# Expert weights slot by slot instead of in groups of four slots, in a Mamba-2, GLA and PEER trunk layer on one Trainium2 core

## The chip, the cores and the metric

The kernel runs on one core of a Trainium2 chip. The metric is the device time of one execution in microseconds; less is better. The names of the engines in the rows: PE is TensorE's matmuls (PEld its weight loads), DVE is VectorE, ACT is ScalarE, POOL is GpSimd, SP is SyncE, which issues transfers only. A q behind a name is the engine's instruction queue.

## The reference

One layer is applied to 1024 new tokens (the prompt) and to 8 single tokens (the samples): a modulated RMSNorm, a mixer (16 Mamba-2 heads beside 4 gated linear attention heads), a residual, a second modulated RMSNorm, and an expert layer (PEER) with its residual and a last RMSNorm. All of it is in 32-bit floats. The change touches the expert layer alone:

```python
def block_fn(xb):                                   # 128 tokens
    qd = (xb @ w_query).reshape(-1, PEER_HEADS, 2, PEER_DQ // 2)
    s1 = jnp.einsum('thd,hkd->thk', qd[:, :, 0], sub_keys1)
    s2 = jnp.einsum('thd,hkd->thk', qd[:, :, 1], sub_keys2)
    v1, i1 = lax.top_k(s1, 16); v2, i2 = lax.top_k(s2, 16)
...                                                 # the best 16 of the 256 sums, for each of 8 heads
    g = jax.nn.softmax(top_s, axis=-1)
    u = expert_down[idx]
    act = jax.nn.gelu(jnp.einsum('thkd,td->thk', u, xb), approximate=False)
    return jnp.einsum('thk,thkd->td', g * act, expert_up[idx])
```

So each token picks 8 x 16 = 128 experts out of 16384. An expert is one row of `expert_down` and one of `expert_up`, 1024 numbers each.

## The kernel before

Five phases follow one another, with a barrier between them: modulation and first norm, the input projections, the mixer for the samples, the mixer for the prompt, and the experts. Each phase has one program per engine, and semaphores tie the programs together; each engine works through its own program in order.

The expert phase (`experts`) goes over the prompt in 8 tiles of 128 tokens, one token per partition, tile 0 written out and tiles 1 to 7 in a hardware loop on each engine, and then over the 8 samples. A tile has 128 **slots**: slot k is the k-th chosen expert of each of the 128 tokens. For each slot

- GpSimd gathers 128 rows, one per token, of 2048 numbers (down row and up row side by side, 8 KB) into one of 8 buffers (`buf`, a ring of `RING = 8`) with one indirect DMA (L1764). It waits for `summed`, which says that the slot eight places earlier has been used up (L1769).
- VectorE multiplies the down halves with the tokens and sums them, one dot per token (`dot`, L1866), as soon as the gather has landed. It increments `dotted`.
- ScalarE turns the dots into weights. `GROUP = 4` slots go together: it waits for the fourth dot of the group (L1835), computes the gelu of all four columns in one instruction (L1836), multiplies each column by its gate (L1838, four instructions), and writes for each slot a diagonal matrix with the 128 weights (L1842, a copy of the identity scaled per partition) into a ring of 8. Each diagonal increments `weighed`. Where ScalarE reads what it has just written, `Chain.step` makes it wait for its own write.
- TensorE waits for `weighed` of the slot and adds diagonal x up halves to two PSUM banks (L1797, two matmuls of 512 columns, which appear as four records). Its last matmul increments `summed`.

Between groups, the same engines do the routing of the next tile in pieces, so many after each group as hand-written tables say (`PE_PIECES`, `ACT_PIECES`, `DVE_PIECES`): TensorE the query products (L1528), the token transposes (L1509) and scores (L1520) after groups 1 to 13; ScalarE the copies out of PSUM (L1544, L1554, L1549) and two exponentials (L1564); VectorE the searches for the best 16 after groups 8 to 27. At the start of a tile, VectorE reads the previous tile's sum out of PSUM after its fourth dot (`fin.add`, f_y, L1662); TensorE's first slot waits for it. ScalarE computes the last norm of the previous tile after group 0 (`fin.scalar`). SyncE loads the tokens (h2) and the residual (x1) of a tile and stores its output (y).

The samples use the same buffers: sample b is one slot of 128 rows, and its dot, gelu (L1857), weights and matmuls (L1815) go slot by slot already.

Of the kernel before, what the change touches and what calls it, by code (L numbers as in the profile page):

```python
# [21 lines left out]
ACT = mybir.ActivationFunctionType  # L22
# [22 lines left out]
SLOTS = PH * TOPK  # L45
RING = 8
GROUP = 4
# [57 lines left out]
class Prog:  # L105
# [31 lines left out]
    def sem(self, name):  # L137
        handle = self.nc.alloc_semaphore(name=name)
        self.sems.append(handle)
        return handle  # L140
# [1551 lines left out]
def drive(pieces, count):  # L1692

    for _ in range(count):
        next(pieces, None)


def experts(g):
# [4 lines left out]
    NG = SLOTS // GROUP  # L1703
    with ExitStack() as st:
# [4 lines left out]
        idx, gate, h2 = sb("idx", [P, SLOTS], U32), sb("gate", [P, SLOTS]), sb("h2", [P, D])  # L1709
        dots, acts, wts = sb("dots", [P, SLOTS]), sb("acts", [P, SLOTS]), sb("wts", [P, SLOTS])  # L1710
# [3 lines left out]
        dotted, wch, weighed, summed = sem("dotted"), sem("wch"), sem("weighed"), sem("summed")  # L1714
# [13 lines left out]
        @block.sync  # L1728
        def _(sp):
            sp.sem_inc(fin.stored, 16)  # L1730
            sp.dma_start(rt.h2[:], g.h2_d[0:P, :]).then_inc(rt.h2_in, 16)
            rt.load_constants(sp)
            sp.dma_start(fin.gate2[:], g.mod_d[NS, 5 * D:6 * D].partition_broadcast(P)).then_inc(fin.consts_in, 16)
            sp.dma_start(fin.final[:], io["norm_final"].partition_broadcast(P)).then_inc(fin.consts_in, 16)

            def store_y(n):
                sp.wait_ge(fin.y_ready, n + 1)
                sp.dma_start(io["y_p"][bass.ds(n * P, P), :], fin.y[:]).then_inc(fin.stored, 16)

            def tile(n, first):  # L1740
                sp.wait_ge(h2_kept, n + 1)
                sp.dma_start(rt.h2[:], g.h2_d[bass.ds(n * P + P, P), :]).then_inc(rt.h2_in, 16)
                if not first:
                    store_y(n - 1)
                sp.dma_start(fin.x1[:], g.x1_d[bass.ds(n * P, P), :]).then_inc(fin.x1_in, 16)

            tile(0, True)
            with sp.Fori(1, NT) as n:
                tile(n, False)
            sp.wait_ge(rt.q_ps, 4 * (NT + 1))  # L1750
            for b in range(NS):
                sp.dma_start(spread(b), g.h2_d[SEQ + b, :].partition_broadcast(P)).then_inc(spread_in, 16)
            sp.wait_ge(fin.sum_read, NT)
            sp.dma_start(fin.gate2[0:NS, :], g.mod_d[0:NS, 5 * D:6 * D]).then_inc(gates_in, 16)
            store_y(NT - 1)
            sp.dma_start(fin.x1[0:NS, :], g.x1_d[SEQ:ROWS, :]).then_inc(fin.x1_in, 16)
            sp.wait_ge(fin.y_ready, NT + 1)
            sp.dma_start(io["y_s"], fin.y[0:NS, :]).then_inc(fin.stored, 16)
            sp.wait_ge(fin.stored, 16 * (NT + 2))
# [60 lines left out]
        @block.scalar  # L1820
        def _(act):
            A = nc.scalar.activation
            own = rt.scalar(act, 0)
            drive(own, 10)
            def tile(n, first):
                ch = Chain(act, wch, n * (2 + 2 * NG))
                route = rt.scalar(act, n + 1)
                for q in range(NG):
                    if q in (0, NG // 2):
                        half = 0 if q == 0 else 1  # L1830
                        gs = slice(half * HALF_SLOTS, (half + 1) * HALF_SLOTS)
                        act.wait_ge(rt.gated, n * 2 + half + 1)
                        ch.step(A(gate[:, gs], rt.gate[:, gs], ACT.Copy))
                    ks = slice(q * GROUP, (q + 1) * GROUP)
                    act.wait_ge(dotted, n * SLOTS + (q + 1) * GROUP)  # L1835
                    ch.step(A(acts[:, ks], dots[:, ks], ACT.Gelu))  # L1836
                    for k in range(q * GROUP, (q + 1) * GROUP):
                        last = A(wts[:, k:k + 1], acts[:, k:k + 1], ACT.Copy, scale=gate[:, k:k + 1])  # L1838
                    ch.step(last)
                    for k in range(q * GROUP, (q + 1) * GROUP):  # L1840
                        act.wait_ge(summed, n * SLOTS + k + 1)
                        A(diag[:, k % RING, :], g.ident[:], ACT.Copy, scale=wts[:, k:k + 1]).then_inc(weighed, 1)  # L1842
                    if first:
                        drive(own, FIRST_ACT_PIECES.get(q, 0))
                    drive(route, ACT_PIECES.get(q, 0))
                    if q == 0 and not first:
                        fin.scalar(act, n - 1, P)

            tile(0, True)
            with act.Fori(1, NT) as n:  # L1850
                tile(n, False)
            act.wait_ge(turn_ps, 1)
            A(turned[:].rearrange("p a b -> p (a b)"), g.bank(2, cols=2 * NS), ACT.Copy).then_inc(turn_kept, 1)
            fin.scalar(act, NT - 1, P)
            for b in range(NS):
                act.wait_ge(s_dotted, b + 1)
                A(wts[:, b:b + 1], dots[:, b:b + 1], ACT.Gelu).then_inc(s_acted, 1)  # L1857
            fin.scalar(act, NT, NS)
# [135 lines left out]
```

## Time and profile before

| | |
|---|---|
| time, median of 3 runs | 4351.11 us (4350.53 to 4353.85) |
| profiled execution, its own time | 4346.83 us |
| its span in the trace | 4345.3 us |
| mean granted TensorE clock | 0.894 of full speed |
| expert slots of the prompt, first to last | about 1398 to 4310 us of the span |
| data moved | 1268.44 MB, of it 1114.83 MB by GpSimd's queue |

An engine's busy time is the time in which its instructions ran. In a row of instructions the tile names stand as out<-in with x and a count, then busy time and mean duration, then the idle time of the engine before these instructions and what ended it. The granted clock is a share of TensorE's full 2.4 GHz; its lower level is 1.2 GHz, 0.50.

### The profile page before, as it was taken

To read this page: it belongs to the slowest core of one execution; us is meant where nothing else is said; L and a number is where in the kernel's file an instruction comes from. 1 tells how busy PE (TensorE), PEld (TensorE's weight loads), DVE (VectorE), ACT (ScalarE), POOL (GpSimd) and SP (SyncE) were. 2 spreads that over 40 slices of the span, in tenths; PEclk is the share of its full clock that TensorE was granted. 3 is DMA by queue.
4 is the path that set the end of the run, shared out by engine and by line. 5 is a ranking of instruction groups with operands and counts; after the bars stand their busy time and mean duration, and the time that the engine had idled before them with its cause. 6 is when DMAs were issued, how large, how long until landed. Compare 5 with 4: busy or idle time off the path is not lost.

```text
span 4345.3 us, 39670 instructions
## 1 busy us (share of the span) xinstructions
PE 3465.6 (80%) x11665; PEld 1919.4 (44%) x11665; DVE 2356.5 (54%) x4736; ACT 1058.9 (24%) x3031; POOL 1357.3 (31%) x1251
## 2 busy tenths in 40 slices
PE   5998994679994987787797787788779778877876
PEld 1997772255553533442353253244335325334432
DVE  4531104556654766467457546646745754664674
ACT  2110112134431222222222222222222222222222
POOL 1110111200000444444344343444434434444342
PEclk8999995789997998898898898889889889989988
DMA  7332212453224999999999999999999999999996
GB/s 289 95 110 102 82 43 93 170 187 105 87 72 192 368 375 364 379 383 373 368 386 375 381 373 371 376 373 379 374 364 393 377 377 380 378 370 378 395 375 265
DMA packets 210786, 1268.44 MB, mean 292 GB/s; under 512 B 26081, under 2 KB 51305, under 8 KB 74138
## 3 DMA queue, kind: packets, MB, share of 16 engines
q0 software_dynamic: 159760, 1114.83, 65.1%
q1 hardware_dynamic: 50834, 151.67, 9.8%
q14 instruction: 147, 1.20, 0.1%
q8 instruction: 45, 0.74, 0.1%
HBM read 1218.12 MB, written 48.29 MB: 291 GB/s over the span
## 4 chain that ended last, share of the span: by engine, by line
PE 27%; DMA 25%; issue 8%; ACT 3%; POOL 3%; DVE 3%; POOLq 0%; ACTq 0%; DVEq 0%; SPq 0%
DMA e_buf<-in_experts,e_idx 25%; PE ps L1797 23%; PE ps L1528 4%; POOL e_buf L1764 3%; ACT e_wts L1838 2%; DVE e_buf L1866 2%; ACT e_diag L1842 1%; ACT e_acts L1836 1%; DMA e_buf<-in_experts,e_idxT 0%; DVE r_row L1617 0%; DVE r_work L1616 0%; DMA r_wq<-in_w_query 0%; POOLq L58 0%; DVE r_work L1613 0%; PE ps L1815 0%
## 5 line engine op out<-in xcount | busy, mean ns | idle before, releaser
L1797 PE MATMUL ps<-e_buf,e_diag 128*128 128x512 f32 x4096 | 2045.7, 658 | 628.3 <-ACT e_diag L1842 627.7
L1866 DVE SCALAR_TENSOR_TENSOR e_buf<-e_buf,e_h 128x1024 f32<-128x1024 f32 x1024 | 1247.7, 1226 | 1098.7 <-DMA e_buf<-in_experts,e_idx 1084.2
L1764 POOL DMA_INDIRECT e_buf<-in_experts,e_idx x1024 | 1200.1, 1172 | 1612.2 <-PE ps L1797 1411.0
L1797 PEld LDWEIGHTS ps<-e_buf,e_diag 128*128 128x128 f32 x4096 | 843.1, 211 | 1759.6 <-issue 999.9
L1836 ACT ACTIVATE e_acts<-e_dots 128x4 f32<-128x4 f32 x256 | 52.6, 205 | 2087.6 <-DVE e_buf L1866 2087.5
L1842 ACT ACTIVATE e_diag<-ident,e_wts 128x128 f32<-128x128 f32 x1024 | 327.2, 390 | 25.8
L1528 PEld LDWEIGHTS ps<-r_h2T,r_wq 128*128 128x128 f32 x2304 | 269.3, 193 | 34.0 <-issue 34.0
L1528 PE MATMUL ps<-r_h2T,r_wq 128*128 128x128 f32 x2304 | 269.9, 276 | 3.0 <-DMA r_wq<-in_w_query 3.0
L856 PE MATMUL ps<-xo_w_out,xo_catT 128*128 128x512 f32 x512 | 224.5, 592 | 1.7 <-DVE xo_x L889 1.7
L1838 ACT ACTIVATE e_wts<-e_acts,e_gate 128x1 f32<-128x1 f32 x1024 | 218.6, 284 | 10.1 <-ACT e_acts L1836 2.2
L74 PE MATMUL ps<-p_wth,hT_high 128*128 128x512 f32 (+1 forms) x432 | 170.6, 395 | 10.9 <-PEq L439 10.9
L76 PE MATMUL ps<-p_wth,hT_low 128*128 128x512 f32 (+1 forms) x432 | 171.0, 396 | 0.0
L75 PE MATMUL ps<-p_wtl,hT_high 128*128 128x512 f32 (+1 forms) x432 | 170.4, 395 | 0.0
L74 PE MATMUL ps<-hT_high,p_wh 128*128 128x344 f32 x480 | 154.7, 322 | 11.4 <-DVE p_wl L69 11.4
L76 PE MATMUL ps<-hT_high,p_wl 128*128 128x344 f32 x480 | 154.2, 321 | 0.0
L75 PE MATMUL ps<-hT_low,p_wh 128*128 128x344 f32 x480 | 154.0, 321 | 0.0
L856 PEld LDWEIGHTS ps<-xo_w_out,xo_catT 128*128 128x128 f32 x512 | 96.7, 190 | 117.6 <-issue 117.2
L907 POOL DMA_DIRECT2D x_d<-xo_x x8 | 4.3, 541 | 411.4 <-DVE xo_x L889 411.4
L64 DVE CAST p_wth<-p_wt 128x4096 fp32r<-128x4096 f32 x6 | 13.8, 2292 | 199.1 <-PE ps L76 190.7
L610 POOL DMA_DIRECT2D proj_d<-p_ev x54 | 31.6, 585 | 280.8 <-ACT p_ev L645 280.8
L645 ACT ACTIVATE p_ev<-ps 128x512 f32<-128x512 f32 (+1 forms) x54 | 32.3, 598 | 280.2 <-PE ps L76 280.2
L74 PEld LDWEIGHTS ps<-hT_high,p_wh 128*128 128x128 f32 x480 | 91.0, 190 | 12.3 <-DVE p_wl L69 12.3
(353 smaller groups left out, 2971.1 us busy)
## 6 DMA issues: line engine op xcount, KB each, us to landing
m_w<-in_w_mod SPq DMA_DIRECT2D x12, 2048.0 KB, 9.0
e_buf<-in_experts,e_idx POOLq DMA_INDIRECT x1024, 9.2
p_wt<-in_w_rows SPq DMA_DIRECT2D x6, 2048.0 KB, 8.3
proj_d<-p_ev POOLq DMA_DIRECT2D x48, 256.0 KB, 2.3
x_zgv<-proj_d SPq DMA_DIRECT2D x8, 1536.0 KB
p_w<-in_w_chan SPq DMA_DIRECT2D x20, 512.0 KB, 4.1
r_wq<-in_w_query SPq DMA_DIRECT2D x4, 2048.0 KB, 14.1
xbc_d<-p_res POOLq DMA_DIRECT2D x12, 516.0 KB, 3.0
```

Source lines behind the costliest of these rows:

```text
L74: nc.tensor.matmul(out, lhsT[0], rhs[0], start=start, stop=False)
L75: nc.tensor.matmul(out, lhsT[0], rhs[1], start=False, stop=False)
L76: return nc.tensor.matmul(out, lhsT[1], rhs[0], start=False, stop=stop)
L645: nc.scalar.activation(evs[n % 6][0:rs, :], g.bank(n % 6, rows=rs), func).then_inc(tevac, 1)
L856: last = g.nc.tensor.matmul(g.bank(cols, rows=rs), self.catT[:, k, 0:rs], self.w[:, k, cols * 512:(cols + 1) * 512], start=(k == 0), stop= ...
L1528: last = nc.tensor.matmul(g.bank(4 + b, cols=P, at=m * P), self.wq[:, b, k, m * P:(m + 1) * P], self.h2T[:, k, :], start=(k == 0), stop=(k ...
L1764: return pool.indirect_dma_start(out=buf[s][:], out_offset=None, in_=io["experts"], in_offset=bass.IndirectOffsetOnAxis(ap=numbers, axis=0 ...
L1797: last = nc.tensor.matmul(g.bank(cols), diag[:, k % RING, :], buf[k % RING][:, D + cols * 512:D + (cols + 1) * 512], start=(k == 0), stop= ...
L1836: ch.step(A(acts[:, ks], dots[:, ks], ACT.Gelu))
L1838: last = A(wts[:, k:k + 1], acts[:, k:k + 1], ACT.Copy, scale=gate[:, k:k + 1])
L1842: A(diag[:, k % RING, :], g.ident[:], ACT.Copy, scale=wts[:, k:k + 1]).then_inc(weighed, 1)
L1866: V.scalar_tensor_tensor(out=down, in0=down, scalar=1.0, in1=row, op0=ALU.mult, op1=ALU.mult, accum_out=out).then_inc(sem, 1)
```

## The change

ScalarE no longer handles four slots at a time. For each slot it waits for that slot's dot, computes the gelu of the one column, multiplies it by the gate, and writes the diagonal; each of the first two is followed by a wait for its own write. The count of such waits per tile rises from 2 + 2 x 32 to 2 + 2 x 128. The routing pieces stay where they were, after every fourth slot, and the other engines' programs are as before.

```diff
             def tile(n, first):
-                ch = Chain(act, wch, n * (2 + 2 * NG))
+                ch = Chain(act, wch, n * (2 + 2 * SLOTS))
...
-                    ks = slice(q * GROUP, (q + 1) * GROUP)
-                    act.wait_ge(dotted, n * SLOTS + (q + 1) * GROUP)
-                    ch.step(A(acts[:, ks], dots[:, ks], ACT.Gelu))
                     for k in range(q * GROUP, (q + 1) * GROUP):
-                        last = A(wts[:, k:k + 1], acts[:, k:k + 1], ACT.Copy, scale=gate[:, k:k + 1])
-                    ch.step(last)
-                    for k in range(q * GROUP, (q + 1) * GROUP):
+                        act.wait_ge(dotted, n * SLOTS + k + 1)
+                        ch.step(A(acts[:, k:k + 1], dots[:, k:k + 1], ACT.Gelu))
+                        ch.step(A(wts[:, k:k + 1], acts[:, k:k + 1], ACT.Copy, scale=gate[:, k:k + 1]))
                         act.wait_ge(summed, n * SLOTS + k + 1)
                         A(diag[:, k % RING, :], g.ident[:], ACT.Copy, scale=wts[:, k:k + 1]).then_inc(weighed, 1)
```

## Rows read from the trace of the kernel before

**Rows 1.** The page: busy time of each engine, share of the span.
```profile
PE 3465.6 (80%) x11665; PEld 1919.4 (44%) x11665; DVE 2356.5 (54%) x4736; ACT 1058.9 (24%) x3031; POOL 1357.3 (31%) x1251
```
**Rows 2.** The page: the chain that ended last, shares by line.
```profile
DMA e_buf<-in_experts,e_idx 25%; PE ps L1797 23%; PE ps L1528 4%; POOL e_buf L1764 3%; ACT e_wts L1838 2%; DVE e_buf L1866 2%; ACT e_diag L1842 1%; ACT e_acts L1836 1%; DMA e_buf<-in_experts,e_idxT 0%; DVE r_row L1617 0%; DVE r_work L1616 0%; DMA r_wq<-in_w_query 0%; POOLq L58 0%; DVE r_work L1613 0%; PE ps L1815 0%
```
**Rows 3.** Busy time by stretch: length, engines, granted clock, DMA share, GB/s.
```profile
1397.93:3928.82 2530.89, 2007.58 (x5648) 976.95 (x5649) 1536.60 (x3497) 637.11 (x2180) 1053.36 (x909) 0.89 0.95 376
2121.85:2280.95 159.10, 135.37 (x508) 76.75 (x507) 85.33 (x185) 42.80 (x142) 65.46 (x57) 0.93 0.96 380
2280.95:2481.99 201.04, 148.38 (x301) 61.53 (x300) 130.72 (x300) 48.54 (x171) 81.54 (x73) 0.89 0.95 376
3273.00:3297.00 24.00, 23.59 (x103) 14.40 (x102) 11.92 (x21) 5.28 (x19) 10.29 (x10) 1.00 1.00 417
2148.00:2164.00 16.00, 9.26 (x23) 4.36 (x22) 6.63 (x11) 3.25 (x10) 4.28 (x5) 0.80 1.02 429
2136.00:2144.00 8.00, 8.00 (x14) 3.21 (x13) 5.21 (x9) 6.01 (x13) 3.50 (x3) 0.71 0.59 218
2176.00:2184.00 8.00, 8.00 (x43) 5.47 (x42) 3.52 (x6) 2.94 (x10) 3.07 (x3) 1.00 0.98 367
4320.00:4328.00 8.00, 5.65 (x12) 0.83 (x12) 4.78 (x12) 0.61 (x3) 0.00 (x0) 1.00 1.01 426
```
**Rows 4.** The chain in order of time: start us, us, what.
```profile
2211.74 10.82 DMA e_buf<-in_experts,e_idx
...
2223.86 0.21 ACT e_acts L1836
...
2224.14 0.15 issue
2224.29 0.66 ACT e_wts L1838 x3
...
2225.51 7.15 PE ps L1797 x16
...
2233.42 10.40 DMA e_buf<-in_experts,e_idx
```
**Rows 5.** Timeline of TensorE in the sample part: start us, us, instruction, idle before.
```profile
4325.85 1.88 PE L1815 MATMUL ps<-e_buf,e_wpad 128*8 128x512 f32 x4 [0.55 <-DVE e_wpad L1906]
4328.28 1.88 PE L1815 MATMUL ps<-e_buf,e_wpad 128*8 128x512 f32 x4 [0.55 <-DVE e_wpad L1906]
```
**Rows 6.** The page: groups of ScalarE, busy and mean ns, then idle before.
```profile
L1836 ACT ACTIVATE e_acts<-e_dots 128x4 f32<-128x4 f32 x256 | 52.6, 205 | 2087.6 <-DVE e_buf L1866 2087.5
L1842 ACT ACTIVATE e_diag<-ident,e_wts 128x128 f32<-128x128 f32 x1024 | 327.2, 390 | 25.8
...
L1838 ACT ACTIVATE e_wts<-e_acts,e_gate 128x1 f32<-128x1 f32 x1024 | 218.6, 284 | 10.1 <-ACT e_acts L1836 2.2
```
**Rows 7.** Timeline at the start of tile 2.
```profile
2121.03 0.70 DVE L1876 COPY e_h<-r_h 128x1024 f32<-128x1024 f32 x1 [3.90 <-issue]
...
2132.69 1.22 DVE L1662 TENSOR_TENSOR f_y<-ps,f_gate 128x1024 f32<-128x1024 f32 x1
...
2134.46 17.03 PE L1797 MATMUL ps<-e_buf,e_diag 128*128 128x512 f32 x32 [8.51 <-ACT e_diag L1842]
...
2145.41 0.95 POOL L1764 DMA_INDIRECT e_buf<-in_experts,e_idx  x1 [0.77 <-PE ps L1797]
```
**Rows 8.** Timeline of TensorE amid the router's pieces, tile 2.
```profile
2179.18 3.73 PE L1528 MATMUL ps<-r_h2T,r_wq 128*128 128x128 f32 x32
2182.75 7.03 PE L1797 MATMUL ps<-e_buf,e_diag 128*128 128x512 f32 x16
2189.62 3.73 PE L1528 MATMUL ps<-r_h2T,r_wq 128*128 128x128 f32 x32
...
2210.80 1.05 PE L1520 MATMUL ps<-r_keys,r_qT 128*128 128x128 f32 x8
```
**Rows 9.** The page: DMA issues of the gathers, median us to landing.
```profile
e_buf<-in_experts,e_idx POOLq DMA_INDIRECT x1024, 9.2
```

## Prediction

> **What bounds the kernel now.** The page's engine line first [rows 1]: no engine is full over the span (PE 80%, with matmuls of which part ran at half clock; VectorE 54%, ScalarE 24%). The chain that ended last [rows 2] is mostly two things in turn, transfers of gathered experts (25%) and the L1797 matmuls (23%), with ScalarE and GpSimd pieces between. A chain that alternates like this is a loop through several engines, so I read the time of one turn.
>
> The stretches [rows 3] give the size: seven tiles take 2530.89 us, 361.6 us a tile, 2.82 us a slot, at 376 GB/s. A slot gathers 128 rows of 8 KB, 1.049 MB. DMA share is 0.95 there, which looks full, but the share does not measure what is left: at shares of 1.00 to 1.02 the same engines moved 417, 429 and 426 GB/s, and at 0.98 only 367. Where a tile starts and little is left to fetch, 8 us fall to 218.
>
> The chain in order of time [rows 4] shows the turn. The gather issued at 2211.74 lands after 10.82 us; then its dot, one gelu, three further gate products, the first diagonal, and 16 matmuls (the four slots of the group), 7.15 us, until GpSimd issues the gather that reuses this buffer, at 2233.42. That is 21.68 us for a ring of eight slots: 2.71 us a slot. Eight transfers back to back, spaced as in the sample part, where nothing holds the gathers up (2.43 us from one slot's matmuls to the next) [rows 5], need only 19.4 us. So the ring is the limit, not the transfer: a group keeps four buffers of eight until its fourth dot is there.
>
> **The change, part by part.** *Removed:* the wait of slots 0 to 2 of a group for slot 3, and batching. On the turn in [rows 4] three gate products (0.66 us) leave the path before the first diagonal, and of the 16 matmuls 12 (three quarters of 7.15, 5.36 us) have been done while the later transfers landed. The turn falls from 21.68 to about 15.7 us, under the 19.4 us that eight transfers need. The transfers themselves become the limit; the spare 3.7 us becomes queueing, so issue-to-landing, now a median of 9.2 us [rows 9], should rise to about 13 us.
>
> *Added on ScalarE:* gelu of one column instead of four. A 4-column one takes 205 ns [rows 6]; 96 more a tile, 768 in all, are 157 us of busy time, and each gate product now waits for its own gelu (0.15 us of "issue" in [rows 4], some 0.1 ms in all if every one counted). Cover: ScalarE sat idle 2087.5 us for dots [rows 6]. A slot will cost it 0.2 + 0.28 + 0.39 plus about 0.3 of waits, 1.2 us of the 2.5 available. Were the cover gone, the price would be those 157 us and the waits. Queued behind the new wait for each dot are the later diagonals, the router's copies and exponentials and the finishing norm; all of these already stood behind the group's last dot, so none gets later, nor do PE and VectorE, which wait for them. The added waits for the chain semaphore are on ScalarE's own results only.
>
> *Moved:* the gathers, which GpSimd issues as buffers come free. One issue is a DMA_INDIRECT of about 0.95 us after a wake-up of 0.77 [rows 7], 1.72 us a slot; it fits in 2.5.
>
> *What is late next.* PE: a slot is four records of 0.43 us, 1.72 (7.03 for 16 in [rows 8]); with the router's 3.73 us pieces groups take 10.44 us back to back, 2.61 a slot, PE-bound even now. Per tile 128 x 1.72 plus about 35 of router (8 x 3.73 and 5 x 1.05) is 255 us. Slots 0 to 55, which carry all of the router's PE work, need 56 x 1.72 + 35 + about 3 for a cold start, 134 us; they now take 159.10 [rows 3]. The other 72 slots have 24% slack. VectorE: 85.33 + 130.72 = 216 us a tile [rows 3]. Both stay under the transfers.
>
> *Rate of transfers.* The lower bound is 2.43 us a slot [rows 5], the upper the loop's present 2.71. I take the 24 us stretch at 417 GB/s in which ten gathers were issued [rows 3], since it has the flow that the changed kernel needs: 1.049/417 = 2.515 us. Three further transfers of 0.52 MB a tile (h2, x1, y) add 3.8 us at that rate.
>
> *Tile start.* PE may not write slot 0 before VectorE has read the old sum (f_y, after the dot of slot 3) [rows 7]. Neither that nor the loop's jump (3.90 us before the copy of h2) changes. PE then starts cold: 17.03 us for eight slots [rows 7] against 13.8. Today the transfers lose 8 x (1 - 218/417) = 3.8 us there [rows 3]; between 0 and 3.8 remain, because the ring is then full up to slot 7, and I take 3.
>
> *Sum.* A tile: 128 x 2.515 + 3.8 + 3 = 328.7 us, 32.9 less than 361.6. Eight tiles: 263 us. The profiled execution took 4346.8 us; 4346.8 - 263 = 4084. The median of the runs, 4351.1, is 4 us higher, so I forecast 4088 us. Bounds: 128 x 2.43 + 3.8 = 314.8, eight times 46.8 less, 3977; and 128 x 2.71 + 7.6 = 354.5, 57 less, 4294.
>
> *The skill against the row.* The stage averages 376 GB/s and holds 429 for 16 us [rows 3]. The Trainium skill, "DMA: Bandwidth & Descriptors", section Bandwidth ("Where 436 GB/s comes from"), says that HBM limits one core to about 358 GB/s; by that a slot would take 2.93 us, more than now, and nothing could be won. The trace disagrees at every stretch that has transfers queued.
>
> **The rivals.** *Transfers hold at about their present pace* even with a full queue, since each issue costs them something: for it speaks 367 GB/s at share 0.98 in 8 us with three issues [rows 3]; against it 417 with ten issues in 24 us. At 2.66 us a slot a tile takes 340.5 + 6.8 = 347.3, 114 us less: 4237. It decides above 2.60 us.
>
> *No change:* the transfer is the bound already, as the 0.95 share suggests, and freed buffers only lengthen the queue. That gives 4351. Against it speaks the 2.71 us turn with 19.4 of 21.7 us needed.
>
> *Slower: TensorE's clock.* Groups now give runs of four slots; single slots leave PE a gap after each 1.72 us. At 1.2 GHz a slot takes 3.44 us. With 255 us of PE work a tile at 2.4 GHz, PE passes 361.6 us when over 42% of that work runs at the lower level; the granted 0.89 [rows 3] means 22% of the time now. At half, a tile is 382 us, 164 us more in all: 4515. Against it: in the sample part PE ran 1.88 us, paused 0.55, and kept a granted clock of 1.00 [rows 3, 5], and the long waits behind the present cold starts go away. The Trainium skill, "TensorE: Matmul & The Clock Gate", section "A second HAM failure mode: psum-queue depth-cycling", warns that micro-idles between matmul groups make the clock swing between its levels; [rows 5] shows it holding, though only for some 14 us.
>
> **How the numbers follow.** Forecast (2.43 to 2.60 us a slot; own range 4010 to 4170): 0.74. Present pace, partly gained: 0.13. No change: 0.06. Clock: 0.07. Faster by over 0.2% (about what a measurement of this kernel can tell): 0.74 + 0.13 = 0.87; same 0.06; slower 0.07. The range 3995 to 4265 leaves out the last two cases and about 0.03 at either end of the first two.
>
> **What would show it.** Right: issue-to-landing near 13 us, the stage above 405 GB/s, VectorE's waits for gathers spaced about 2.45 us, fewer matmuls released by ScalarE after long idles, granted clock over 0.89, 1024 gelus of about 0.2 us. The chain should be mostly transfers, with PE only in the router's groups. Wrong: a stage still at 375 GB/s with a longer landing (rivals one and two), or mean L1797 records above 658 ns and a lower granted clock (rival three). What I trust least is a sustained 417 GB/s, seen only for tens of microseconds.

## The result, and the profile after

The changed kernel takes 4043.44 us (median of 6 runs, 4041.51 to 4045.71), the one before 4351.09 us on the same chip (6 runs): 0.9292 of the time, 95% interval 0.928 to 0.9304, or 308 us less. The profiled executions took 4346.83 and 4042.96 us, 304 less.

The page of the changed kernel, busy time of each engine:

```profile
PE 3361.8 (83%) x11665; PEld 1849.0 (46%) x11665; DVE 2348.0 (58%) x4736; ACT 1376.9 (34%) x3799; POOL 1415.7 (35%) x1251
```

Its groups of instructions; busy us and mean ns, then idle before and what ended it (L1863 is the dot, L1839 the diagonal, L1837 the gate product):

```profile
L1797 PE MATMUL ps<-e_buf,e_diag 128*128 128x512 f32 x4096 | 1954.8, 627 | 424.2 <-ACT e_diag L1839 351.1
L1863 DVE SCALAR_TENSOR_TENSOR e_buf<-e_buf,e_h 128x1024 f32<-128x1024 f32 x1024 | 1239.7, 1225 | 815.4 <-DMA e_buf<-in_experts,e_idx 799.7
...
L1836 ACT ACTIVATE e_acts<-e_dots 128x1 f32<-128x1 f32 x1024 | 207.3, 202 | 1445.5 <-DVE e_buf L1863 1443.8
L1839 ACT ACTIVATE e_diag<-ident,e_wts 128x128 f32<-128x128 f32 x1024 | 411.0, 401 | 34.0
L1837 ACT ACTIVATE e_wts<-e_acts,e_gate 128x1 f32<-128x1 f32 x1024 | 301.5, 294 | 34.2 <-ACT e_acts L1836 1.1
```

ScalarE is now busier by 155 us of gelus, as counted. Its whole busy time rose by 318 us (1058.9 in [rows 1]): the gate products and the diagonals, which followed one another directly in a group and overlapped, now cost 83 and 84 us more (218.6 and 327.2 in [rows 6]). It still sits idle 1443.8 us for dots, where it was 2087.5 [rows 6].

Busy time by stretch in the changed kernel (columns as in [rows 3]): seven tiles, one tile, and six microseconds at that tile's start.

```profile
1393.85:3663.42 2269.57, 1928.72 (x5656) 921.77 (x5656) 1528.89 (x3497) 915.34 (x2852) 1104.26 (x912) 0.95 1.00 420
2363.92:2688.88 324.96, 272.73 (x808) 130.74 (x808) 215.03 (x485) 131.00 (x408) 156.99 (x130) 0.95 1.00 419
...
2373.00:2379.00 6.00, 6.00 (x13) 2.51 (x12) 3.93 (x6) 5.40 (x7) 1.86 (x2) 0.82 0.50 184
```

A tile takes 2269.57/7 = 324.2 us, where it took 361.6; the transfers run at 420 GB/s on average, where they ran at 376 [rows 3]. The eight tiles, from the first dot of the first to the first dot of the samples, account for 300 of the 304 us; the other 4 us lie ahead of the first dot, in phases that the change doesn't touch. They are within the scatter: over all runs of this case the first dot starts between 1391 and 1399 us of the span.

The chain in order of time, changed kernel, one turn of the ring in tile 3:

```profile
2562.29 10.70 DMA e_buf<-in_experts,e_idx
...
2574.28 0.21 ACT e_acts L1836
2574.52 0.30 ACT e_wts L1837
2574.84 0.41 ACT e_diag L1839
2575.30 2.00 PE ps L1797 x4
...
2578.06 14.48 DMA e_buf<-in_experts,e_idx
```

From issue to the reissue of the same buffer this turn takes 15.77 us, where [rows 4] took 21.68: four matmul records stand on it, not sixteen, and one gate product, not four. In both turns the gather lands after nearly the same time (10.70 and 10.82 us), so they can be compared; the part from landing to reissue fell from 10.86 to 5.07 us. It is not the average turn: that is eight times a slot's share of a tile, 8 x 324.2/128 = 20.3 us, where it was 22.6, because most gathers now wait in the queue, as the next one on this chain does (14.48 us). The page's row of the gathers (median us from issue to landing) says the same for all 1024:

```profile
e_buf<-in_experts,e_idx POOLq DMA_INDIRECT x1024, 13.0
```

It was 9.2 [rows 9]. The gathers are not slower, since 420 GB/s are moved for 376: they wait longer in a queue that now runs dry only in places (a DMA share of 1.00 over the seven tiles, 0.50 in the six microseconds at a tile's start).

### The profile page after: what moved, and what is told of

It is laid out like the page before. It is cut to its first block, busy times and chain, and to the rows that moved or that the text cites. A ratio compares the mean times of both kernels' runs of the same rounds, so it can differ in the third digit from the quotient of the medians.

```text
span 4041.4 us, 42774 instructions
## 1 busy us (share of the span) xinstructions
PE 3361.8 (83%) x11665; PEld 1849.0 (46%) x11665; DVE 2348.0 (58%) x4736; ACT 1376.9 (34%) x3799; POOL 1415.7 (35%) x1251
## 4 chain that ended last, share of the span: by engine, by line
PE 25%; DMA 24%; DVE 7%; issue 6%; POOL 3%; ACT 2%; POOLq 0%; DVEq 0%; SPq 0%; ACTq 0%
DMA e_buf<-in_experts,e_idx 23%; PE ps L1797 20%; PE ps L1528 5%; POOL e_buf L1764 3%; DVE e_buf L1863 2%; DVE r_pos L1576 1%; ACT e_diag L1839 1%; DVE r_work L1581 1%; DVE r_row L1617 1%; DVE r_work L1616 1%; ACT e_wts L1837 0%; DVE r_iu L1576 0%; DVE r_work L1613 0%; DMA e_buf<-in_experts,e_idxT 0%; DVE r_top L1572 0%
## 5 line engine op out<-in xcount | busy, mean ns | idle before, releaser
L1797 PE MATMUL ps<-e_buf,e_diag 128*128 128x512 f32 x4096 | 1954.8, 627 | 424.2 <-ACT e_diag L1839 351.1
L1863 DVE SCALAR_TENSOR_TENSOR e_buf<-e_buf,e_h 128x1024 f32<-128x1024 f32 x1024 | 1239.7, 1225 | 815.4 <-DMA e_buf<-in_experts,e_idx 799.7
L1764 POOL DMA_INDIRECT e_buf<-in_experts,e_idx x1024 | 1257.6, 1228 | 1272.5 <-PE ps L1797 1051.2
L1797 PEld LDWEIGHTS ps<-e_buf,e_diag 128*128 128x128 f32 x4096 | 779.6, 199 | 1525.9 <-issue 781.2
L1836 ACT ACTIVATE e_acts<-e_dots 128x1 f32<-128x1 f32 x1024 | 207.3, 202 | 1445.5 <-DVE e_buf L1863 1443.8
L1839 ACT ACTIVATE e_diag<-ident,e_wts 128x128 f32<-128x128 f32 x1024 | 411.0, 401 | 34.0
L1837 ACT ACTIVATE e_wts<-e_acts,e_gate 128x1 f32<-128x1 f32 x1024 | 301.5, 294 | 34.2 <-ACT e_acts L1836 1.1
L64 DVE CAST p_wth<-p_wt 128x4096 fp32r<-128x4096 f32 x6 | 13.8, 2293 | 198.8 <-PE ps L76 190.6
```

Source lines behind the costliest of these rows:

```text
L1764: return pool.indirect_dma_start(out=buf[s][:], out_offset=None, in_=io["experts"], in_offset=bass.IndirectOffsetOnAxis(ap=numbers, axis=0 ...
L1797: last = nc.tensor.matmul(g.bank(cols), diag[:, k % RING, :], buf[k % RING][:, D + cols * 512:D + (cols + 1) * 512], start=(k == 0), stop= ...
L1836: ch.step(A(acts[:, k:k + 1], dots[:, k:k + 1], ACT.Gelu))
L1837: ch.step(A(wts[:, k:k + 1], acts[:, k:k + 1], ACT.Copy, scale=gate[:, k:k + 1]))
L1863: V.scalar_tensor_tensor(out=down, in0=down, scalar=1.0, in1=row, op0=ALU.mult, op1=ALU.mult, accum_out=out).then_inc(sem, 1)
```

## The experiments

My theory: a group's wait keeps four of eight buffers occupied, the turn of the ring is then longer than eight transfers, and the transfers idle. Rivals: ScalarE's batch ahead of the first diagonal was the delay; ScalarE's late start alone was the loss; the gain came from TensorE's higher clock. Times are to be compared as ratios to the kernel before on the same chip: it took 4339.31 us beside the first four runs, 4336.5 beside the next four, 4351.03 beside the last.

**Pairs.** Groups of two on ScalarE, from the kernel before.

```diff
-                    act.wait_ge(dotted, n * SLOTS + (q + 1) * GROUP)
+                    for j in range(q * GROUP, (q + 1) * GROUP, 2):
+                        act.wait_ge(dotted, n * SLOTS + j + 2)
...
```

> Groups of two slots on ScalarE instead of four; all else as before the change. Held buffers set the pace (my theory): the turn of the ring for the slot that closes a group is 21.7 us with four; with two it loses two gate products (0.44 us) and eight matmuls (3.6 us), so 17.7 us, still under the 19.4 us of eight transfers. So nearly all of the gain should be there: 4045 to 4090 us, gathers landing some 11 to 12 us after their issue, over 405 GB/s. Rival (each slot handled on its own is what pays, gain in proportion to the slots freed from waiting: a slot waits for 1.5 others on average with four, for 0.5 with two, so two thirds of 308 us): 4145 us.

4050.54 us, ratio 0.9337 (0.9321 to 0.9353); the gathers land after 11.1 us. Its seven tiles:

```profile
1398.63:3672.32 2273.69, 1909.10 (x5656) 926.43 (x5656) 1529.06 (x3497) 730.29 (x2404) 1075.59 (x911) 0.95 1.00 419
```

A tile takes 324.8 us, for 324.2 with single slots. Nearly the whole gain is there with groups of two, as the turn predicts (17.7 us by the working above, under 19.4), and not two thirds of it. So what counts is on which side of the transfers' 19.4 us the turn lies, not how long a slot waits.

**The fourth dot.** The changed kernel's single instructions, but the group's wait is back.

```diff
-                        act.wait_ge(dotted, n * SLOTS + k + 1)
+                        act.wait_ge(dotted, n * SLOTS + (q + 1) * GROUP)
```

> The changed kernel's single gelu, gate product and diagonal per slot, but the first slot of a group waits for the group's fourth dot as before. Theory (held buffers): the turn loses only some 0.5 us of 21.7 (the first diagonal no longer stands behind three gate products), 2.65 us a slot for 2.71, so 4280 to 4350 us, landing near 9 us, about 380 GB/s. Rival (the batch of gate products ahead of the first diagonal was the delay): near 4043 us.

4287.68 us, ratio 0.9891 (0.9863 to 0.9918), in the range of the theory. The rival, near 4043 us, fell.

**The fourth diagonal.** ScalarE slot by slot, but TensorE waits for the group.

```diff
-                    pe.wait_ge(weighed, n * SLOTS + k + 1)
+                    pe.wait_ge(weighed, n * SLOTS + (k // GROUP + 1) * GROUP)
```

> The changed kernel, but TensorE starts a group only when the group's fourth diagonal is written; ScalarE works slot by slot. Theory (buffers are held until TensorE has read them): ScalarE's early start frees none, the turn is about 21.2 us, 4280 to 4350 us, landing near 9 us. Rival (ScalarE's late start alone was the loss): 4043 to 4100 us.

4268.65 us, ratio 0.9836 (0.982 to 0.9853), just under the lower end that I gave. This rival fell too. In both, the gathers land after 9.3 us. The chain in order of time of the run with the fourth dot, two turns:

```profile
2589.38 10.48 DMA e_buf<-in_experts,e_idx
...
2602.25 8.72 PE ps L1797 x16
...
2611.73 10.08 DMA e_buf<-in_experts,e_idx
...
2624.19 7.15 PE ps L1797 x16
...
2632.10 10.06 DMA e_buf<-in_experts,e_idx
```

The turns are 22.35 and 20.37 us; sixteen matmul records stand on each, as before the change. Either half of the slot-by-slot work alone is worth 1.1% or 1.6%; both together 7%. A buffer comes free only when every stage of its slot has run early, so the gains do not add up: one wait for the group, wherever it stands, holds all four buffers.

**A ring of four.** The changed kernel with four buffers for the prompt; the ring of diagonals shrinks to four with them. The edit's main lines:

```diff
-        PER = 16 * (SLOTS // RING)
+        FEW = 4
+        PER = 16 * (SLOTS // FEW)
...
-                    gather(k % RING, idx[:, k:k + 1]).then_inc(landed[k % RING], 16)
+                    gather(k % FEW, idx[:, k:k + 1]).then_inc(landed[k % FEW], 16)
...
-            pe.sem_inc(summed, RING)
+            pe.sem_inc(summed, FEW)
...
```

> The changed kernel with a ring of four buffers for the prompt instead of eight. Theory: the turn of one buffer without any queueing is dot 1.3, gelu to diagonal 1.1, matmuls 2.0, wake-up 0.8 and about 5.5 from issue to landing when alone, 10.7 us, over the 9.7 us that four transfers need, and each of the router's pieces on TensorE and VectorE adds its full length to it. So slot by slot must lose its gain: 2.7 to 3.4 us a slot, 4250 to 4900 us, landing 5 to 7 us, under 380 GB/s. Rival (working slot by slot keeps the transfers full whatever the number of buffers): under 4100 us.

4892.8 us in one run, at the upper end of the range; the transfers run at 316 GB/s over seven tiles and the gathers land after 7.5 us, more than the 5 to 7 that I gave. The chain in order of time:

```profile
2608.72 8.08 DMA e_buf<-in_experts,e_idx
...
2619.11 2.00 PE ps L1798 x4
2621.87 7.73 DMA e_buf<-in_experts,e_idx
...
2635.67 5.89 DMA e_buf<-in_experts,e_idx
...
2646.63 8.56 DMA e_buf<-in_experts,e_idx
```

Turns of 13.15, 13.80 and 10.96 us for four slots, 2.7 to 3.5 us a slot. The rival, under 4100 us, fell. Slot by slot is no merit in itself: with half the buffers the same code is slower than the kernel that the change started from.

**TensorE kept busy.** The kernel before, with idle work for TensorE after groups 14 to 31. It tests the clock.

```diff
                         drive(route, PE_PIECES.get(k // GROUP, 0))
+                        if k // GROUP > 13:
+                            for _ in range(2):
+                                nc.tensor.matmul(g.bank(3), g.ident[:], rt.keys[:, 0:4, :].rearrange("p u r -> p (u r)"),
+                                                 start=True, stop=True)
```

> The kernel before with TensorE given idle work: after each of groups 14 to 31, where its pauses between groups are longest, it does two extra 128x512 matmuls of constants into an unused PSUM bank (1.7 us at 2.4 GHz); nothing reads them. It tests whether the changed kernel won by its higher granted clock (0.93 against 0.89). Theory (held buffers): the clock rises some, the stage keeps its turn, within 1% of before, 4300 to 4370 us. Rival (the clock is what was won: the L1797 records were 91 us less busy in the changed kernel, and a clock near 1.0 would win up to 285 us): 4060 to 4250 us.

4289.19 us, ratio 0.9888 (0.9854 to 0.9922), a little more gain than the 1% I allowed, and short of the rival's 4060 to 4250. Its stage by stretch, and its L1797 group:

```profile
1400.00:4250.00 2850.00, 2454.37 (x7042) 1195.84 (x7042) 1748.35 (x3973) 732.58 (x2499) 1201.77 (x1036) 0.94 0.96 381
```

```profile
L1797 PE MATMUL ps<-e_buf,e_diag 128*128 128x512 f32 x4096 | 1956.6, 634 | 423.0 <-ACT e_diag L1846 422.8
```

The granted clock is 0.94 here and 0.95 in the changed kernel, and the expert matmuls are busy 1957 us in the one and 1955 in the other; yet the transfers stay at 381 GB/s and the time falls by 47 us, not by 308. So a clock of that height is worth about 15% of the gain where groups still hold the buffers. That is about what the turn gives: the matmuls of one group out of two stand on it, so half of the 89 us by which they are less busy (2045.7 us before the change), 45 us. What the changed kernel would lose at the old clock was not tried.

**The sum read early.** The changed kernel, with the read of the old sum moved ahead of the first dot.

```diff
+                if not first:
+                    dve.wait_ge(summed, n * SLOTS + RING)
+                    fin.add(dve, n - 1, P)
                 for k in range(SLOTS):
...
-                    if k == GROUP - 1 and not first:
-                        dve.wait_ge(summed, n * SLOTS + RING)
-                        fin.add(dve, n - 1, P)
```

> The changed kernel, but VectorE reads the previous tile's sum out of PSUM before the first dot of the new tile instead of after its fourth. In the changed kernel TensorE waits 10.4 us for that read while it holds all eight buffers, and the transfers fall under 100 GB/s for 3 to 4 us. Theory (what is left to win is where the ring still starves): seven tile starts times about 3.5 us, 1.0062 to 0.6% less, 4010 to 4030 us. Rival (the transfers are full as it is and the moved 2.5 us of VectorE delays the dots): 4043 us or more.

4040.62 us, ratio 0.9317 (0.929 to 0.9343): no gain over the changed kernel. The 8 us at the start of tile 3, first in this run, then in the changed kernel:

```profile
2372.00:2380.00 8.00, 7.54 (x16) 3.05 (x15) 3.70 (x6) 7.64 (x17) 5.16 (x4) 0.88 0.93 338
```

```profile
2372.00:2380.00 8.00, 7.71 (x15) 3.53 (x16) 4.99 (x8) 6.34 (x12) 2.77 (x2) 0.80 0.62 240
```

The dip became shallower there, but the tile's time stayed: 324.67 us for 324.96, and 324.2 us in both as the mean of seven tiles. The expectation fell. In the first 40 us of tile 3, from its first dot on, the transfers run at 399 GB/s for 371; in the rest of the tile they run at 422 for 426. So the start's gain is given back later in the tile; why the rest is slower stays open.

**The sum read early, and a lump of VectorE split.** To the run with the sum read early (the "run before the last" below), one edit is added: in `DVE_PIECES` the entry `17: 4` becomes `17: 2, 18: 2`.

> The run before the last with one thing more: the four router pieces of VectorE after group 17 (6.7 us in one lump, after which gathers dip to 200 to 370 GB/s in the changed kernel) are split, two after group 17 and two after group 18. Theory: about 1 to 2 us a tile more is won than by the early sum alone, 3995 to 4022 us. Rival (the ring covers the lump): the same as with the early sum alone.

4045.82 us, ratio 0.9326 (0.93 to 0.9352). Nothing is won by it either, and this expectation fell as well; the time is what the rival gives, that the ring covers that lump.

**ScalarE's work doubled.** The changed kernel with every gelu and every gate product done twice.

```diff
                         ch.step(A(acts[:, k:k + 1], dots[:, k:k + 1], ACT.Gelu))
+                        ch.step(A(acts[:, k:k + 1], dots[:, k:k + 1], ACT.Gelu))
                         ch.step(A(wts[:, k:k + 1], acts[:, k:k + 1], ACT.Copy, scale=gate[:, k:k + 1]))
+                        ch.step(A(wts[:, k:k + 1], acts[:, k:k + 1], ACT.Copy, scale=gate[:, k:k + 1]))
```

> The changed kernel with every gelu and every gate product done twice, each with its wait: 2048 more instructions on ScalarE, some 0.55 us more per slot before its diagonal. Theory (ScalarE's per-slot work is covered, the ring has about 3.7 us to spare per turn): the same, 4035 to 4060 us. Rival (ScalarE's per-slot cost is on the path): up to 1024 x 0.55 = 563 us more; a tenth of it on the path would be 4100 us.

4057.28 us, ratio 0.9355 (0.9329 to 0.9382). The two added groups on ScalarE:

```profile
L1839 ACT ACTIVATE e_wts<-e_acts,e_gate 128x1 f32<-128x1 f32 x1024 | 301.2, 294 | 33.7
L1837 ACT ACTIVATE e_acts<-e_dots 128x1 f32<-128x1 f32 x1024 | 207.7, 203 | 32.4
```

509 us of added busy time and 66 of waits cost 0.9355 - 0.9292 = 0.6% of 4351, some 27 us; the two intervals leave room for 11 to 44. By the tiles it is less: 326.0 us a tile for 324.2, 15 us over eight. So some 3 to 5% of the added work is on the path. If the same share holds for the 318 us that the change itself added on ScalarE (an estimate, not measured), they cost 10 to 15 us.

**Eights.** Groups of eight, the whole ring.

```diff
-                    act.wait_ge(dotted, n * SLOTS + (q + 1) * GROUP)
-                    ch.step(A(acts[:, ks], dots[:, ks], ACT.Gelu))
+                    if q % 2 == 0:
+                        ks = slice(q * GROUP, (q + 2) * GROUP)
+                        act.wait_ge(dotted, n * SLOTS + (q + 2) * GROUP)
+                        ch.step(A(acts[:, ks], dots[:, ks], ACT.Gelu))
...
```

> Groups of eight slots on ScalarE, the whole ring, instead of four; the router's pieces of both old groups follow the eight. Theory (the turn of the ring): 21.7 us with four plus four more gate products (0.9 us) and sixteen more matmuls (7.15 us) is 29.8 us for eight slots, 3.7 us a slot: 8 x 128 x 3.7 + 1434 us outside the stage = 5220 us, range 5000 to 5400; landing near 9 to 15 us since the whole ring is issued at once. Rival (the loss grows in proportion to the slots that a slot waits for, 3.5 on average for 1.5 with four, at 205 us for each): 4340 + 411 = 4750 us.

5689.51 us in one run, above the range that I gave. The chain in order of time, one turn, and a stretch at the start of its matmuls:

```profile
2995.61 12.32 DMA e_buf<-in_experts,e_idx
...
3009.66 1.41 ACT e_wts L1839 x7
...
3011.62 16.39 PE ps L1797 x32
...
3028.78 14.10 DMA e_buf<-in_experts,e_idx
```

```profile
3012.00:3014.00 2.00, 2.00 (x3) 0.80 (x3) 0.00 (x0) 2.00 (x7) 0.00 (x0) 0.50 0.01 4
```

The turn is 33.17 us, 4.15 a slot: 1024 x 4.15 + 1434 = 5684, which is the time. The rival's 4750 is far off. My size was off too: I had given 32 matmul records 14.3 us and they take 16.39, since TensorE, idle for 16.99 us before, starts them at a granted clock of 0.50 (0.80 is the mean over the span), and the transfer took 12.32 us for 10.82.

## Why the prediction was right, point by point

- **The ring's turn is the limit, not the transfers.** Right. The turns for groups of one, two, four and eight (15.77, 17.7 by working, 21.68 and 33.17 us) order the times: 4043, 4051, 4351 and 5690 us, nearly flat while the turn is under 19.4 us and rising with it above. Four buffers instead of eight undo the gain, and either wait for the group by itself takes most of it back.
- **The turn falls to 15.7 us.** 15.77 in the chain, on a turn whose gather landed as fast as the one in [rows 4].
- **Landing after about 13 us.** 13.0, and partly luck: the working adds the spare time of one turn (3.7 us, with a landing after 10.82) to the median landing of all (9.2), and takes 19.4 us for eight transfers where 20.3 were measured. With that pace it would have given 13.8.
- **ScalarE's added work is covered.** Right to within 3 to 5% of it. The gelus were counted rightly (155 us for 157), but the gate products and diagonals, which no longer overlap, added another 167 us of busy time that the working put at nothing.
- **Rate of transfers, 2.515 us a slot.** The mis-sized term, though by little. I had 328.7 us a tile, it is 324.2; the 4.5 us, eight times, are 36 of the 45 us by which the time is under the forecast's 4088. Another 4 lie ahead of the first dot, and 4 had been added for the distance from the profiled execution to the median, which is 0.5 us in the changed kernel. A tile moves 134.2 MB of experts and 1.6 MB besides; at 324.2 us that is 419 GB/s, the tile's start included (the row shows 420). The start itself was sized rightly: at 184 GB/s for 6 us against 420 it loses 3.4 us, for 3. So the rest of the tile runs at 135.8 MB in 320.8 us, 423 GB/s or 2.48 us a slot, where I took 417 from a busy stretch of the old kernel.
- **The rival of transfers that hold their pace under one issue per slot** fell: 420 GB/s with an issue every 2.5 us. What held the eight microseconds at 367 GB/s that spoke for it, no run shows. The Trainium skill ("DMA: Bandwidth & Descriptors", Bandwidth, "Where 436 GB/s comes from") gives about 358 GB/s per core, half of the memory's 716, as what binds such transfers. This trace disagrees: the one core that runs here moved 420 GB/s for 2270 us on end.
- **The rival of the clock** went the other way: the granted clock rose from 0.89 to 0.95. Before, TensorE was idle for 628 us ahead of 256 groups, 2.5 us each on average; in the changed kernel it is idle for 424 us ahead of 1024 slots, 0.4 us each. With extra matmuls in the old kernel's pauses the clock was 0.94, and with groups of eight, where 17 us of idle time stood before the matmuls shown, 0.80 over the span.
- **One sign that did not come.** The chain that ended last should have been mostly transfers, with TensorE only in the router's groups. The page of the changed kernel:

```profile
DMA e_buf<-in_experts,e_idx 23%; PE ps L1797 20%; PE ps L1528 5%; POOL e_buf L1764 3%; DVE e_buf L1863 2%; DVE r_pos L1576 1%; ACT e_diag L1839 1%; DVE r_work L1581 1%; DVE r_row L1617 1%; DVE r_work L1616 1%; ACT e_wts L1837 0%; DVE r_iu L1576 0%; DVE r_work L1613 0%; DMA e_buf<-in_experts,e_idxT 0%; DVE r_top L1572 0%
```

It was 25% transfers and 23% L1797 before [rows 2]. The limit changed and these shares hardly did, so they do not tell whether the ring or the transfers set the pace; the length of a turn and the landing time did.

## What to carry to other kernels

With a ring of buffers, walk one turn from issue to reissue in the chain and set it against the number of buffers times the time of one transfer; whichever was longer gave the pace of the kernels with eight buffers here to within 5%, whatever the busy shares said. Walk a turn whose transfer did not queue long: with a full queue the landing time grows until the turn equals the pace. A batch anywhere between landing and release adds its whole length to the turn, and taking it out at one engine is worth little while the next engine still waits for the batch (1.1% and 1.6% here, for 7%). Once the turn is below the transfers, shortening it further wins next to nothing: pairs did as well as single slots to within half a per cent.

## What the runs showed of the hardware that was not expected

- A DMA share of 0.95 to 0.96 stood beside 376 to 381 GB/s, and 1.00 beside 420. The share said 5% of room where there was 12%.
- Extra matmuls that nobody reads made the kernel before 1.1% faster (0.9888); the granted clock of the stage rose from 0.89 to 0.94, and the expert matmuls were 89 us less busy.
- Removing a visible dip in the transfers (240 to 338 GB/s over 8 us of a tile) gained nothing measurable over the tile.
